# One fp32 gMLP layer by seven block products: the MLP's input turned by VectorE, the first loads and products in another order

## The reference

```python
hn = rms_norm(x, norm1_g)
z = gelu(hn @ w_in)                         # w_in 1024 x 4096
u, v = split(z)                             # 2048 each
v = layer_norm(v) * ln_g                    # then, in chunks of 128 tokens and 8 groups,
sv = einsum('gts,bnsge->bntge', tril(w_s), v) + b_s
x = x + (u * sv) @ w_out                    # w_out 2048 x 1024
x = x + square(relu(rms_norm(x, norm2_g) @ w1)) @ w2   # w1 1024 x 4096, w2 4096 x 1024
return rms_norm(x, final_g)
```

## Time and profile before

| | |
|---|---|
| median of 3 runs | 1124.58 us (1124.0 to 1125.15) |
| profiled execution | 1126.03 us, its span 1124.2 us |
| TensorE busy | 1114.8 us, 99% of the span |
| VectorE, ScalarE busy | 785.9 us (70%), 569.4 us (51%) |
| mean granted TensorE clock | 0.998 |
| matmul instructions | 5088 |

### The profile page before, as it was taken

One profiled execution on the slowest core, in us unless ns is written; L12 is line 12 of the kernel. 1 busy time (PEld: TensorE's weight loads), 2 busy tenths in 40 slices (PEclk: granted clock), 3 DMA queues, 4 the chain that ended last, 5 costly groups with the idle time before them and its releaser, 6 DMA issues.

```text
span 1124.2 us, 13090 instructions
## 1 busy us (share of the span) xinstructions
PE 1114.8 (99%) x5088; PEld 928.2 (83%) x5088; DVE 785.9 (70%) x833; ACT 569.4 (51%) x870; POOL 23.5 (2%) x17
## 2 busy tenths in 40 slices
PE   8999999999999999999999999999999999999997
PEld 7888888888888888888888888888888888888886
DVE  4976655688779986678658547455599575677666
ACT  6774444553554334565774365454653433433456
POOL 0000000000000000000000000000000000000240
PEclk9999999999999999999999999999999999999999
DMA  8173253272865494731353635527878354343213
GB/s 294 45 210 127 94 187 113 75 244 93 316 250 221 159 358 144 217 113 38 113 187 126 211 113 183 193 108 272 293 292 305 111 226 187 113 150 113 78 73 150
DMA packets 81933, 193.80 MB, mean 172 GB/s; under 512 B 4528, under 2 KB 10704, under 8 KB 75216
## 3 DMA queue, kind: packets, MB, share of 16 engines
q1 hardware_dynamic: 81392, 192.69, 48.7%
q10 hardware_dynamic: 480, 0.28, 0.1%
HBM read 134.24 MB, written 58.72 MB: 172 GB/s over the span
## 4 chain that ended last, share of the span: by engine, by line
PE 98%; DMA 1%; ACT 0%; DVE 0%; ACTq 0%; issue 0%
PE banks L427 32%; PE banks L432 32%; PE banks L431 32%; PE banks L496 3%; PE banks L541 1%; DMA gain_rows<-in_a_ln_g_dram 1%; DVE rows L1516 0%; ACT spare L1133 0%; PE banks L503 0%; PE banks L552 0%; PE banks L523 0%; ACT rows L1325 0%; ACT o_rms L1333 0%; ACTq L922 0%; ACTq L924 0%
## 5 line engine op out<-in xcount | busy, mean ns | idle before, releaser
L984 ACT ACTIVATE pair_high<-left_and_right 128x1024 fp32r<-128x1024 f32 x168 | 177.2, 1060 | 244.4 <-PE banks L427 193.4
L1378 DVE TENSOR_TENSOR ring_low<-left_and_right,ring_high 128x512 fp32r<-128x512 f32 x224 | 152.6, 692 | 192.7 <-ACT ring_high L954 192.3
L1386 DVE TENSOR_TENSOR pair_low<-left_and_right,pair_high 128x1024 fp32r<-128x1024 f32 x168 | 204.1, 1230 | 113.9 <-ACT pair_high L984 113.9
L954 ACT ACTIVATE ring_high<-left_and_right 128x512 fp32r<-128x512 f32 x224 | 138.4, 629 | 251.2 <-PE banks L427 155.9
L427 PE MATMUL banks<-pair_high 128*128 128x512 f32 x672 | 261.9, 390 | 0.0
L432 PE MATMUL banks<-pair_high,pair_low 128*128 128x512 f32 x672 | 261.5, 389 | 0.0
L431 PE MATMUL banks<-pair_low,pair_high 128*128 128x512 f32 x672 | 261.4, 389 | 0.0
L427 PE MATMUL banks<-s_high,ring_high 128*128 128x512 f32 x384 | 149.6, 389 | 0.0
L431 PE MATMUL banks<-s_low,ring_high 128*128 128x512 f32 x384 | 149.4, 389 | 0.0
L432 PE MATMUL banks<-s_high,ring_low 128*128 128x512 f32 x384 | 149.4, 389 | 0.0
L427 PEld LDWEIGHTS banks<-pair_high 128*128 128x128 f32 x672 | 126.1, 188 | 26.6 <-DVE pair_low L1386 0.3
(11 more groups left out here) (116 smaller groups left out, 1223.5 us busy)
## 6 DMA issues: line engine op xcount, KB each, us to landing
left_and_right<-sums SPq DMA_DIRECT2D x40, 1024.0 KB, 7.1
left_and_right<-in_mlp_w_dram SPq DMA_DIRECT2D x36, 1024.0 KB, 6.5
sums<-rows SPq DMA_DIRECT2D x34, 1024.0 KB, 5.4
left_and_right<-in_a_w_in_dram SPq DMA_DIRECT2D x19, 1024.0 KB, 6.2
v_blocks<-rows SPq DMA_DIRECT2D x8, 1024.0 KB, 4.5
left_and_right<-in_a_w_out_dram SPq DMA_DIRECT2D x8, 1024.0 KB, 9.7
rows<-in_x_dram SPq DMA_DIRECT2D x7, 1024.0 KB, 8.7
spare<-v_blocks SPq DMA_DIRECT2D x6, 1024.0 KB, 6.9
```

The costliest lines, as they stand in the source:

```text
L954: nc.scalar.activation(ring_high[k][:, :], right_place(n, pos)[:, k, :], ACT.Copy)\
L984: nc.scalar.activation(pair_high[pair_entry(d, pos, k)][:, :, :], pair_of(d, pos, k), ACT.Copy)\
L1378: nc.vector.tensor_tensor(ring_low[k][:, :], right_place(n, pos)[:, k, :], ring_high[k][:, :].bitcast(F32), ALU.subtract).then_inc(low_don ...
L1386: nc.vector.tensor_tensor(pair_low[e][:, :, :], pair_of(d, pos, k), pair_high[e][:, :, :].bitcast(F32), ALU.subtract).then_inc(low_done, 1)
```

## The change

- **y.** `turn(4, ...)` is gone. a12 and a22 go to VectorE too, but not through DRAM: `move_quads` copies a block from `rows` straight into 32-row pieces, 16 DMAs of 64 KB. SP issues all 16 for a12 (from c11) and 8 for a22 (from c21); ACT's own queue issues the other 8 for a22. `turn_y` now makes four instructions of 128 by 512 for a block. The gain is no longer multiplied on ScalarE (but for a11): it is folded into the sums s3, s2 and s4 (`sum_turned`) and into the high and low parts of a12 and a22 (`high_turned`, `low_turned`). All of w1 is loaded in the order 4p + j.
- **s2** of singles 0 and 4 is made, rounded and split by k-tiles (`s2_step`, `high_step`, `low_step`, `sum_turned`), so that a unit waits for a quarter and not for the whole.
- **Start.** The gains other than norm1's are turned later, in single 1 beside the spatial weights. Eight identity products run in three lots (4, 2, 2) instead of eleven in two. The first unit is written by halves (`first_unit`): four products high·high, which wait only for the high parts, then four with the low left part, then four with the low right part.
- **Loads.** The first weight block is loaded in tiles 0, 1 and 2 to 3 instead of 0 and 1 to 3; b21 is loaded ahead of the fourth block of x (a22). The mask of the spatial weights on POOL waits until single 0's last right sum is made. On ScalarE two `split_high` pairs of single 0 stand ahead of `square_x` and of the eviction of a22.

```diff
+        def move_quads(eng, b, blk, dst, quadrants):
+            for q in quadrants:
+                for r in range(4):
+                    eng.dma_start(dst[32 * q:32 * q + 32, r:4 * QT:4, :],
+                                  block_of[blk][32 * r:32 * r + 32, :, P * q:P * q + P]).then_inc(quads_landed[b], 16)
...
+            def first_unit():
+                pe.wait_ge(combo_high, 1)
+                pe.wait_ge(high_done, unit(0, 0, 0) + 1)
...
+                pe.wait_ge(combo_low, 1)
...
+                pe.wait_ge(low_done, unit(0, 0, 0) + 1)
...
-                        if n == 4 and pos == 0 and k == 1:
-                            turn(4, "a22", set_of(slot(4, 1)))
...
-                        if d == 0 and pos == 6 and k == 5:
-                            turn(4, "a12", set_of(slot_double(0, 5)))
...
-            warm(2 * WARM_UP)
+            warm(4)
             turn_g1()
+            warm(2)
             first_turn(0)
             first_turn(1)
-            turn_gains()
-            warm(3)
+            warm(2)
...
                     y_final(sp, "c11")
+                    move_quads(sp, "a12", "c11", quad_a12, range(4))
                     sp.dma_start(y_of("c11"), block_of["c11"]).then_inc(y_stored["c11"], 16)
...
                     y_final(sp, "c21")
+                    sp.wait_ge(low_done, unit_double(0, 6, 7) + 1)
+                    move_quads(sp, "a22", "c21", quad_a22, (0, 1))
+                    sp.wait_ge(quads_landed["a22"], 256)
                     sp.dma_start(y_of("c21"), block_of["c21"]).then_inc(y_stored["c21"], 16)
...
                 elif n == 4:
-                    high_combo(4, "a12")
+                    high_turned("a12")
                     split_high(4, 1, 0)
-                    evict_turned(4, "a22", set_of(slot(4, 1)))
+                    y_final(act, "c21")
+                    act.wait_ge(low_done, unit_double(0, 6, 7) + 1)
+                    move_quads(act, "a22", "c21", quad_a22, (2, 3))
                     split_high(4, 1, 1)
                     square_rows(0, "c21", y_sq, y_squared)
...
-                nc.vector.transpose(dst[:, :, :].rearrange("p j t -> p (j t)"),
-                                    src[:, :, :].rearrange("p t (i j) -> p j t i", j=4)).then_inc(y_turned, 1)
+                for j in steps:
+                    nc.vector.transpose(dst[:, j, :], src[:, :, j:P:4]).then_inc(y_turned, 1)
...
+            def sum_turned(s, steps=range(4)):
...
+                    nc.vector.scalar_tensor_tensor(out=out[:, k, :], in0=left[:, k, :], scalar=gain[:, k:k + 1],
+                                                   in1=right[:, k, :], op0=ALU.mult, op1=op).then_inc(combo_sum, 1)
```

More of the change, by code:

```diff
@@ L22 @@
 QT = NB // P
-WARM_UP = 4
 EPS = 1e-6
@@ L35 @@
 COMBOS = ["a12", "s2", "s1", "s3", "s4", "a22"]
+STEPPED = {0: ["a11", "s2"], 4: ["a11", "a12", "s2", "a22"]}
 REGIONS = ["a11", "a12", "a22", "s2", "s3", "s4", "s1"]
@@ L291, in trunk @@
         g2_landed = sem("g2_landed")
-        quads_landed = {b: sem(f"quads_landed_{b}") for b in ("a11", "a21", "a12")}
+        quads_landed = {b: sem(f"quads_landed_{b}") for b in ("a11", "a21", "a12", "a22")}
         y_turned = sem("y_turned")
         y_scaled = sem("y_scaled")
+        g2_negated = sem("g2_negated")
         v_stored = {b: sem(f"v_stored_{b}") for b in BLOCKS}
@@ L511, in turn_gains @@
             def turn_gains():
-                pe.wait_ge(gains_landed, 32)
-                begin_fill("gains", 7)
-                rest = KT + JT
-                nc.tensor.transpose(ps[:, 7, 0:rest], gain_rows[:, :], ident[0:rest, 0:rest]).then_inc(full[7], 1)
+                pe.wait_ge(gains_landed, 16)
+                bank = other_set(1)[1]
+                begin_fill("gains", bank)
+                nc.tensor.transpose(ps[:, bank, 0:JT], gain_rows[:, :], ident[0:JT, 0:JT]).then_inc(full[bank], 1)
             def first_turn(k):
@@ L1272, in double @@
                         square_rows(0, "c11", y_sq, y_squared)
-                    if pos == 6 and d == 0:
-                        evict_turned(4, "a12", set_of(slot_double(0, 5)))
                     for k in range(4):
@@ L1452, in low_combo, with turn_y @@
                                         ALU.subtract).then_inc(combo_low, 1)
-            def turn_y(blk):
-                i, src, dst = {"a11": (0, quad_a11, raw_a11), "a21": (1, quad, raw_a21), "a12": (2, quad, raw_a12)}[blk]
-                dve.wait_ge(quads_landed[blk], 64)
+            def turn_y(blk, steps=range(4)):
+                src, dst = {"a11": (quad_a11, raw_a11), "a21": (quad_a21, raw_a21), "a12": (quad_a12, raw_a12),
+                            "a22": (quad_a22, raw_a22)}[blk]
+                dve.wait_ge(quads_landed[blk], 64 if blk in ("a11", "a21") else 256)
@@ L1615, in single @@
                     split_low(0, 1, 1)
-                    sum_combo(0, "s2")
                     split_low(0, 1, 2)
+                    for k in range(4):
+                        s2_step(k)
                     split_low(0, 1, 3)
                 elif n == 4:
-                    add_rows(0, 6)
-                    low_combo(4, "a12")
+                    low_turned("a12")
+                    split_low(4, 1, 0)
                     sum_t(4, 0)
-                    split_low(4, 1, 0)
                     split_low(4, 1, 1)
-                    sum_combo(4, "s2")
+                    for k in range(2):
+                        turn_y("a22", [k])
+                        sum_turned("s2", [k])
                     split_low(4, 1, 2)
@@ L1819, in double @@
                         turn_y("a11")
+                    if d == 0 and pos == 6:
+                        turn_y("a21")
                     for k in range(4, 8):
```

269 lines of the change are left out of this document (173 added, 96 removed).

## The result

| | runs | median (lowest to highest) |
|---|---|---|
| after | 14 | 1126.54 us (1124.11 to 1129.05) |
| before, on the same chip | 14 | 1124.72 us (1124.0 to 1125.88) |

The ratio is 1.0015, 95% interval 1.0008 to 1.0022: the change costs 1.8 us. The forecast was 1.8 us less. The time is inside the 8 in 10 range (1119.8 to 1127.0), above the forecast's own (1121.0 to 1125.3) and on the wrong side of before. The 1.8 us is under the 2.2 us that the prediction took for a difference, but the interval of the ratio does not touch 1. The profiled execution of after took 1125.58 us, its span 1123.5.

A forecast was written before the change was run, and what follows sets the result against it. TensorE, busy 99% of the span, was taken as the bound. Terms -3.5 + 0.24 (gains' turn moved) - 1.6 + 3.1 = -1.8 took the profiled 1126.03 to 1124.3; the median, 1.45 lower, 1122.8 us (8 in 10: 1119.8 to 1127.0).

The forecast's parts named there:

- The turns, -3.5: Output projection to MLP: taking y's two turns, 1.75 us each, off TensorE saves 3.5 us.
- The start, -1.6: Kernel start: first product at 8.4 instead of 9.49, plus 0.5 from less half clock; 1.6 us won (0.6 to 3.4).
- Both covers hold: Single 0: x's fourth block lands 0.5 us before TensorE comes, and s2's first k-tile needs only a quarter of the splitting.
- The passage, 3.1 us of stall: Passage to the MLP: VectorE's transposes make TensorE wait 3.1 us, mostly before s1; bounds 2.0 to 5.5.
- Half clock behind the stall: Rival: after the s1 wait, some 3 us at half clock add 1.6 us, giving 1124.4; chance 0.08.
- The wait stands among full units: The prediction's argument against a clock fall behind the s1 wait in the passage; no size given.
- The late pieces: Rival: a22's DMA pieces issue at 0.9 and land 6.4 us later; stall 8.9, sum +4.0, 1128.6 us; chance 0.15.
- the plain pace: Rival: VectorE's quarter transposes cost 0.60 us like plain operations; stall 1.7, sum -3.2, 1121.4 us; chance 0.06.
- the trace disagrees: Remark against the skill's transpose pace on VectorE: 2048 columns took 3.83 us, a plain operation 2.29.
- the fixed part of 1.54: Rival: each VectorE transpose has 1.54 us fixed excess, a quarter costs 2.1; sum +2.8, 1127.4 us; chance 0.04.

The follow-up runs named there:

- before_again: The kernel before, unchanged, run for a second profile; 1124.11 us (1 run).
- pe_a22: The kernel after with only a22 of y turned by TensorE again, its sixteen DMAs gone; 1122.90 us, ratio 0.9982 to before.
- s1_loads: The kernel after with s1 of single 4 in four steps and x's fourth block loaded ahead of b21 again; 1123.97 us, ratio 0.9990 to before.
- loads_back: The kernel after with x's fourth block loaded ahead of b21 again and ScalarE's old order in single 0; 1126.17 us, ratio 1.0008 to before.
- only_a12_2: Repeat of the kernel after with a22 turned by TensorE, a12 by VectorE, and before's start and x load order; 1122.00 us, ratio 0.9975 to before.
- s1_old_start: The kernel after with s1 of single 4 in four steps and before's start and x load order; 1124.16 us, ratio 0.9997 to before.
- old_head: The kernel after with before's start: gains turned at the start, first unit by banks; 1126.05 us, ratio 1.0013 to before.
- again: The kernel after, unchanged, timed and profiled once more; 1126.27 us, ratio 1.0013 to before.
- after_third: The kernel after, unchanged, run for a third profile; 1128.19 us (1 run).

## Why the prediction was wrong

- **The turns, -3.5: right as far as tested.** For a12 it is 1.95 against a turn read in steps of 4 (99.31 against 101.26) and 1.80 against before; I had 1.75. It is kept only where VectorE has room, and for a22 it was never seen by itself.
- **The start, -1.6: the step that failed first.** The mechanism came (first product 7.33, forecast 8.4), the gain did not. I took 9.49 and the clock of the earlier trace rows for how before always starts. Its second profile starts at 9.03 at full clock and reaches the first marker at 461.86; after's three profiles reach it at 462.03, 462.88 and 462.94. My own sum held the sign: I set the median 1.45 us under the profiled execution, and then took 1.6 us from the start of that same execution, which is most likely the same time counted twice. "Both covers hold" failed as well: x's fourth block was awaited for 0.5 us, 1.5 and 1.7, and ScalarE's eviction for 0.8 each time. I had put the landing at 24.4 and TensorE's arrival at 24.9; TensorE came at about 23.0 to 23.2, since the 24.9 was counted from the slow execution's 26.52 and before_again has 24.48; and in pe_a22, with the same load order, had to wait until 24.50. Where the landing is early, the next one in line is late (1.94 us in s1_loads). This step alone took 1.6 us from the sum. The first product itself came earlier than forecast (7.33, not 8.4), for a reason that I had named: the norm1 gain had landed by 3.6, so the two identity products cost nothing.
- **The passage, 3.1 us of stall: right in kind, too small.** The cause and the form of the waits came as written: some tenths at two units of s2, and one of about 2 us at s1. One of 0.68 came a position earlier, at T + 16.9, where I had none. Their sum is 3.8. By passages a22 on VectorE costs 3.03 more than on TensorE (102.34 against 99.31), where 3.1 - 1.75 = 1.35 was forecast; with a turn at 1.95 it lost 5.0, of which the waits show 3.8, and the restart behind each of the four adds about 0.23; the last 0.2 no wait shows. With the shorter issues of loads_back the 3.03 is 2.29. Two sizes were off. ScalarE's eight issues took 6.9 us, not 3.8. I had their landing at T + 11.6 and it came at T + 12.4; and I had not reckoned with the weight's rounding behind them on ScalarE, for which VectorE waited 1.16, until the same moment. And a transpose of 128 by 512 took 1.14 from its start to the next one's (515.75 to 516.89), not 0.95; the fused step was as forecast (0.67, to 517.56).
- **Half clock behind the stall: the rival with 0.08 that came.** Its size was right: 1.5 and 1.7 us (103.84 and 104.04 against 102.34), 1.6 at equal issues, forecast 1.6. It came in two of three profiles. "The wait stands among full units" was no argument against it.
- **The late pieces did not come:** landing 2.1 us, not 6.4. **Nor the plain pace:** 1.08 us for 512 columns, where a plain operation takes 0.69. The Trainium skill, "Vector Engine (DVE) Microarchitecture Reference", section 3.8, has the transposing front end at one element a cycle per lane. No run here reaches that pace, but none can tell the front end from the reading either: in both kernels every transpose reads its source in steps of four elements (in after `src[:, :, j:P:4]`), and the plain operations do not. My "the trace disagrees" was too strong. **Nor the fixed part of 1.54:** four quarters are 4.3 us, and the whole was 3.83; as a fixed part that is 0.16 an instruction.

Put together by traces, after against the second profile of before: start +0.17, passage +1.23, spans 1123.5 against 1122.1. With the fall it is +1.02 and +2.73, spans 1125.9 against 1122.1. The measured median, +1.8, lies between. My sum of -1.8 had -1.6 that was not there, and 1.6 to 3.1 too little of stall and clock: the passage was forecast at -0.4 (3.1 - 3.5) and came at +1.23 to +2.73.

The rule that speaks against the change held for one block and not for the other. The Trainium skill, "VectorE: DVE Perf Modes", "Rules for kernel authors", gives a 128 by 128 transpose to TensorE where the bank is welcome as its place. Here a12 on VectorE wins 1.8 to 2 us, since its work is issued early and meets an engine with room, and a22, in the fullest stretch, loses 2.3 to 3, and 1.6 more when the clock falls.

**Open.** With s1 by steps, a22 on VectorE costs 0.6 to 1.6 us in the passage (99.88 to 100.92 against 99.31, by the length of ScalarE's issues), but 2.2 in the medians (1124.16 against 1122.00) and 1.8 for the other pair (1123.97 against 1122.14). About 0.5 more lies behind the second marker, and it goes with the steps: from there to the end of the span it is 559.6 to 559.7 us in the four profiles with s1 in steps (for instance 1122.4 - 562.81 = 559.6) and 559.1 to 559.2 in the fourteen others (1119.8 - 560.63 = 559.2 in only_a12_2). Its cause was not looked for. Together that is 1.1 to 2.1 us, which reaches the medians if the timed runs lie at the long end of the issues; only profiled executions show the issues, so that is not shown. It was not tried to issue all of a22's pieces from SP. At the pace of a12's sixteen (10.4 us from the first issue, then 2.1 to land) the last would land near 519.9 instead of 515.7, an estimate from the trace of after. Fewer and larger pieces were not tried either.

## What to carry to other kernels

Where one engine bounds and another has a third of its time free, look at that third's place: the same transfer of work won 2 us where the engine had room and lost 2.3 to 3 where it was full, and only doing one half at a time showed it. A DMA issue is work of the engine that issues it, and everything queued behind is late by it: here the passage grew by as much as the issues did. Read a short wait or a low clock in one profiled execution twice before putting it into a sum: a second profile of the kernel before would have taken 1.6 us out of this forecast.

## What the hardware showed that was not expected

- A copy of 64 KB from SBUF to SBUF landed 2.1 us after its issue (median); issuing it took 0.60 us on SP and 0.69 on ScalarE, more than the 0.49 for the pieces from DRAM (that is the median of `quad` in the earlier trace rows). Eight in a row on ScalarE took from 5.50 to 6.98 us in the nine profiles that have them.
- TensorE's clock fell from 2.4 to 1.2 GHz behind single waits. Behind the s1 wait, in a full stream of products, it was low for about 3 us and cost 1.5 to 1.7 us; in s1_old_start it was low for over 6 us. In the profiles it fell behind waits of 1.8 (gains, before), 1.9 (raw_a, s1_loads), 2.3 (gains, s1_old_start) and 2.1 (s1: old_head, again, after_third), and not behind 2.1 in after and in loads_back, nor behind 1.7 (x's rows, after_third). The same wait can do it or not.
